# Sample attention and output mix in one block, with page numbers read earlier and the output weights in freed page strips

## The reference

```
p = rmsnorm(x) @ w_in                      # conv input, q, 3 x (k, v), gates
conv = silu(layernorm(depthwise_conv31(glu)))
o = g0 * compressed_attention(q, k_c, v_c) \
  + g1 * selected_attention(q, top-16 blocks of the paged cache, own tokens) \
  + g2 * window_attention(q, last 512 positions)
x = x + concat(rmsnorm(conv), rmsnorm(o)) @ w_out      # "mix"
h = rmsnorm(x);  x = x + hier_moe(h)                    # 4 groups x 8 experts, top 2
y = rmsnorm(x)
```

## Time and profile before

| | us |
|---|---|
| median of three runs | 1673.9 |
| profiled execution, its own time | 1674.98 |
| its span | 1672.9 |
| TensorE busy in the span | 1410.1 (84%) |
| DVE / ACT / POOL busy | 671.6 / 372.2 / 204.6 |
| sample attention block, from its first matmul | 713.80 to 787.81 |
| mix block | 789.97 to 959.93 |
| DMA over the span | 203 GB/s from and to HBM |

### The profile page before, as it was taken

One profiled execution on the slowest core, in us unless ns is written; L12 is line 12 of the kernel. 1 busy time (PEld: TensorE's weight loads), 2 busy tenths in 40 slices (PEclk: granted clock), 3 DMA queues, 4 the chain that ended last, 5 costly groups with the idle time before them and its releaser, 6 DMA issues. The chain is left out here.

```text
span 1672.9 us, 22422 instructions
## 1 busy us (share of the span) xinstructions
PE 1410.1 (84%) x7518; PEld 829.5 (50%) x7518; DVE 671.6 (40%) x1315; ACT 372.2 (22%) x802; POOL 204.6 (12%) x363
## 2 busy tenths in 40 slices
PE   5999999679899888863799806999999999999950
PEld 4665444479556656633355504544455444544420
DVE  3497788520588777661122391111011101111008
ACT  4000111331456554531011200111111111111103
POOL 0000111462400000042000001111111111111101
PEclk9999999879589999976799957999999999999985
DMA  8500000383430000064311025999999999999917
GB/s 275 226 13 1 19 16 19 128 293 113 152 102 2 2 1 2 1 177 121 148 63 64 33 119 215 402 405 405 402 398 402 405 396 387 395 396 390 398 38 287
DMA packets 81239, 326.63 MB, mean 195 GB/s; under 512 B 12319, under 2 KB 46240, under 8 KB 63042
## 3 DMA queue, kind: packets, MB, share of 16 engines
q1 hardware_dynamic: 65130, 287.51, 43.8%
q0 software_dynamic: 15952, 38.14, 6.6%
q10 hardware_dynamic: 80, 0.01, 0.0%
HBM read 310.95 MB, written 29.45 MB: 203 GB/s over the span
## 5 line engine op out<-in xcount | busy, mean ns | idle before, releaser
L1976 PE MATMUL ps<-arena 128*128 128x512 f32 x544 | 240.3, 598 | 0.0
L1976 PEld LDWEIGHTS ps<-arena 128*128 128x128 f32 x544 | 102.1, 190 | 137.2 <-issue 137.1
L540 DVE SCALAR_TENSOR_TENSOR arena<-arena 128x1024 f32<-128x1024 f32 x120 | 147.5, 1283 | 1.2
L373 PE MATMUL ps<-arena 128*128 128x512 f32 (+1 forms) x384 | 141.2, 527 | 0.0
L1637 PE MATMUL ps<-arena 128*128 128x512 f32 x256 | 115.6, 605 | 15.0 <-DVE arena L1752 15.0
L1984 PE MATMUL ps<-arena 128*64 128x256 f32 x1088 | 121.2, 380 | 0.0
L327 PE MATMUL ps<-arena 128*128 128x352 f32 x384 | 116.8, 465 | 3.3 <-issue 2.9
L2028 PE MATMUL ps<-arena 128*128 128x512 f32 x272 | 119.6, 591 | 0.0
L1112 ACT ACTIVATE arena<-ps,arena 128x640 f32<-128x640 f32 (+7 forms) x128 | 89.8, 701 | 111.1 <-DVE arena L1189 104.2
L1017 PE MATMUL ps<-arena 128*128 128x128 f32 x528 | 88.5, 292 | 20.4 <-DVE arena L1207 9.8
L373 PEld LDWEIGHTS ps<-arena 128*128 128x128 f32 x384 | 72.0, 189 | 67.1 <-issue 61.6
(11 more groups left out here) (369 smaller groups left out, 1584.2 us busy)
## 6 DMA issues: line engine op xcount, KB each, us to landing
arena<-in_w_gate SPq DMA_DIRECT2D x34, 2048.0 KB, 9.4
arena<-in_w_up SPq DMA_DIRECT2D x34, 2048.0 KB, 13.9
arena<-in_w_down SPq DMA_DIRECT2D x34, 2048.0 KB, 13.5
arena<-in_x_prompt SPq DMA_DIRECT2D x16, 512.0 KB, 6.5
arena<-in_cache_cmp SPq DMA_DIRECT2D x64, 128.0 KB, 5.7
arena<-in_cache_cmp POOLq DMA_DIRECT2D x64, 128.0 KB, 5.7
arena<-in_cache_sel SPq DMA_DIRECT2D x64, 128.0 KB, 2.5
arena<-scratch_y SPq DMA_DIRECT2D x16, 512.0 KB, 5.9
```

The source lines that it names most:

```text
L373: mm = pe.matmul(ps[:n, b + o // 512, 0:w], xT[:, k, t * P:t * P + n], w_tm[:, k, o:o + w], start=(k == 0), stop=(k == KT_ - 1))
L540: ins = dve.scalar_tensor_tensor(o, i, dw[:, c, j:j + 1], o, ALU.mult, ALU.add)
L1976: mm = pe.matmul(ps[:, bank, :], xgT_l[:, k, :], w[LARGE][:, k, :], start=(k == 0), stop=(k == KT_ - 1))
```

## The change

Sample attention and mix become one block. `reuse_semaphores()` moves from between them to the boundary ahead of the prompt attention, and SP waits for `own_block` at the end of the block before that. SP and POOL read the page numbers of half 1 at the end of their streams in the prompt attention block and keep them in registers (`late_places`). In the sample part, the `earlier` table is loaded first, the window pages in two DMAs (keys, values), 12 of the 16 pages of `spare_values` at the start, and the values of sequence 3 by both SP and POOL. On TensorE, `scores(1, c)` and `win_scores(1)` come before `sel_values(0)`; PSUM banks change accordingly.

`w_out` is now stored as strips of 128 columns: the second half in the key strips of pages 32 to 63, issued by SP once all scores of half 1 are done (ahead of the last window values and the values of sequence 3), the first half in the value strips of pages 0 to 31, issued after these. `mixT` and `hT` lie in key strips of pages 0 to 31, and `mix` takes `k` in the order 4 to 7, 0 to 3. `ln2` and `ln_final` have semaphores of their own; the first is waited for before the first `h`, the second at the end. The turning and normalising of the sample tokens' attention rows (`turn_sample`, `last_att`, `last_norm`) goes into the mix loop at tiles 0, 2 and 3. The old mix block's functions are otherwise the same and stand in the new block.

```diff
@@ -252,9 +252,10 @@
     return [eng.value_load(page_row[0:1, first + q:first + q + 1], min_val=0, max_val=cache.shape[0] - 1)
             for q in range(PAGES)]
 
-def load_pages(eng, cache, places, into, event, part=slice(0, 256)):
-
-    for q, place in enumerate(places):
+def load_pages(eng, cache, places, into, event, part=slice(0, 256), which=range(PAGES)):
+
+    for q in which:
+        place = places[q]
         eng.dma_start(into(q), cache[bass.ds(place, 1)].rearrange("a p n -> (a p) n")[:, part])\
@@ -693,6 +694,7 @@
         sp.dma_start(own_block, a["consts"][:, o:o + w]).then_inc(sem("own_block_in"), 16)
         cmp_pages(sp, 2, 0)
         cmp_pages(sp, 3, 0)
+        sp.wait_ge(sem("own_block_in"), 16)
 
     @block.tensor
     def _(pe):
@@ -848,6 +850,8 @@
 
 
 
+reuse_semaphores()
+
 att = flat(A4, TILES * 512).rearrange("p (t n) -> p t n", n=512)
 probs = flat(A2b, 3072)
 pT = flat(A3, 3072).rearrange("p (s n) -> p s n", s=3)
 
+late_places = {}
+
 with nc.Block() as block:
     @block.sync
     def _(sp):
         for b in range(4):
             load_pages(sp, a["cache_sel"], page_places(sp, a["cache_sel"], b * PAGES),
                        lambda q, b=b: pages[:, PAGES * b + q, :], f"sel_page{b}")
+        for b in (2, 0, 3):
+            late_places["sp", b] = page_places(sp, a["cache_sel"], HALF + b * PAGES)
 
     @block.tensor
             load_pages(pool, a["cache_sel"], places, lambda q: early_keys(b, q), f"sel_keys{b}", slice(0, P))
+            if b == 1:
+                late_places["pool", 1] = places
+        for b in (2, 3):
+            late_places["pool", b] = page_places(pool, a["cache_sel"], HALF + b * PAGES)
 
     @block.scalar
 CMP_AT, OWN_AT = 0, 64
-WIN_BANK, SMALL_BANK, RANK_BANK, ROW_BANK = 4, 5, 6, 7
+SMALL_BANK, RANK_BANK, ROW_BANK = 5, 6, 7
+WIN_BANK = (4, 6)
 OUT_BANK = (4, 5)
-turned_to = (0, 1, 2, 3, 6, 7)
+turned_to = ((0, 1, 2, 3, 6, 7), (0, 1, 2, 3, 6, 4))
...
+w_out_to = [pages[:, 0:32, P:2 * P], pages[:, 32:64, 0:P]]
+mixT = pages[:, 0:16, 0:P].rearrange("p (s k) n -> p s k n", s=2)
+hT = pages[:, 16:32, 0:P].rearrange("p (s k) n -> p s k n", s=2)
+xt = flat(A1 + 16384, 2048).rearrange("p (s n) -> p s n", s=2)
+h_sb = flat(A3 + 2048, 2048).rearrange("p (s n) -> p s n", s=2)
...
+def w_out(k, o, n):
+
+    return w_out_to[k // 4][:, 8 * (k % 4) + o // P:8 * (k % 4) + (o + n) // P, :]
+
...
+        def load_w_out(part):
+            sp.dma_start(w_out_to[part], a["w_out"][512 * part:512 * part + 512]
+                         .rearrange("(p c) (s m) -> p (c s) m", c=4, m=P)).then_inc(sem(f"w_out_in{part}"), 16)
...
         o, w = const_at["earlier"]
         sp.dma_start(earlier.rearrange("p i j -> p (i j)"), a["consts"][:, o:o + w])\
           .then_inc(sem("earlier_in"), 16)
+        for part in range(2):
+            sp.dma_start(win_pages[:, :, P * part:P * part + P],
+                         a["state_win_use"][0:16, :, P * part:P * part + P].rearrange("s p n -> p s n"))\
+              .then_inc(sem(f"win_page{part}"), 16)
         sp.dma_start(att_g, a["norm_att"].partition_broadcast(P)).then_inc(sem("att_gain_in"), 16)
-        places = page_places(sp, a["cache_sel"], HALF + 2 * PAGES)
         sp.wait_ge(sem("s_scored"), 4)
-        load_pages(sp, a["cache_sel"], places, lambda q: pages[:, 2 * PAGES + q, 0:P], "sel_keys2", slice(0, P))
-        places = page_places(sp, a["cache_sel"], HALF)
+        load_pages(sp, a["cache_sel"], late_places["sp", 2], lambda q: pages[:, 2 * PAGES + q, 0:P], "sel_keys2",
+                   slice(0, P))
         sp.wait_ge(sem("s_win_scored"), 1)
         sp.dma_start(win_pages[:, :, 0:P], a["state_win_use"][16:32, :, 0:P].rearrange("s p n -> p s n"))\
-          .then_inc(sem("win_page"), 16)
-        load_pages(sp, a["cache_sel"], places, lambda q: pages[:, q, 0:P], "sel_values0", slice(P, 2 * P))
-        places = page_places(sp, a["cache_sel"], HALF + 3 * PAGES)
+          .then_inc(sem("win_page0"), 16)
+        load_pages(sp, a["cache_sel"], late_places["sp", 0], lambda q: pages[:, q, 0:P], "sel_values0",
+                   slice(P, 2 * P))
+        sp.wait_ge(sem("s_scored"), 8)
+        load_w_out(1)
         sp.wait_ge(sem("sampled"), 1)
         sp.dma_start(win_pages[:, :, P:2 * P], a["state_win_use"][16:32, :, P:2 * P].rearrange("s p n -> p s n"))\
-          .then_inc(sem("win_values"), 16)
-        load_pages(sp, a["cache_sel"], places, lambda q: pages[:, 3 * PAGES + q, P:2 * P], "sel_values3",
-                   slice(P, 2 * P))
+          .then_inc(sem("win_page1"), 16)
+        load_pages(sp, a["cache_sel"], late_places["sp", 3], lambda q: pages[:, 3 * PAGES + q, P:2 * P],
+                   "sel_values3", slice(P, 2 * P), range(8))
+        load_w_out(0)
+        load_x(0)
+        sp.dma_start(ln2_g, a["ln2"].partition_broadcast(P)).then_inc(sem("ln2_in"), 16)
+        load_x(1)
+        sp.dma_start(w_router, a["w_router"].rearrange("p (k n) -> p k n", k=KT_)).then_inc(sem("w_router_in"), 16)
+        sp.dma_start(final_g, a["ln_final"].partition_broadcast(P)).then_inc(sem("final_gain_in"), 16)
...
     @block.gpsimd
     def _(pool):
-        places = page_places(pool, a["cache_sel"], HALF + 3 * PAGES)
+        def load_values2(which):
+            load_pages(pool, a["cache_sel"], late_places["pool", 2], lambda q: spare_values[:, P * q:P * q + P],
+                       "sel_values2", slice(P, 2 * P), which)
+
+        load_values2(range(0, 12))
         pool.wait_ge(sem("s_scored"), 4)
-        load_pages(pool, a["cache_sel"], places, lambda q: pages[:, 3 * PAGES + q, 0:P], "sel_keys3", slice(0, P))
-        places = page_places(pool, a["cache_sel"], HALF + 2 * PAGES)
-        load_pages(pool, a["cache_sel"], places, lambda q: spare_values[:, P * q:P * q + P], "sel_values2",
-                   slice(P, 2 * P))
-        places = page_places(pool, a["cache_sel"], HALF + PAGES)
-        load_pages(pool, a["cache_sel"], places, lambda q: pages[:, PAGES + q, 0:P], "sel_values1",
-                   slice(P, 2 * P))
+        load_pages(pool, a["cache_sel"], late_places["pool", 3], lambda q: pages[:, 3 * PAGES + q, 0:P],
+                   "sel_keys3", slice(0, P))
+        load_pages(pool, a["cache_sel"], late_places["pool", 1], lambda q: pages[:, PAGES + q, 0:P],
+                   "sel_values1", slice(P, 2 * P))
+        load_values2(range(12, 16))
+        pool.wait_ge(sem("sampled"), 1)
+        load_pages(pool, a["cache_sel"], late_places["pool", 3], lambda q: pages[:, 3 * PAGES + q, P:2 * P],
+                   "sel_values3_pool", slice(P, 2 * P), range(8, 16))
 
...
-            by_batch(half, WIN_BANK, 0, 512, lambda b: win_pages[:, 4 * b:4 * b + 4, 0:P])\
+            pe.wait_ge(sem("win_page0"), 16 * (half + 1))
+            by_batch(half, WIN_BANK[half], 0, 512, lambda b: win_pages[:, 4 * b:4 * b + 4, 0:P])\
                 .then_inc(sem("s_win_scored"), 1)
 
...
                 for b in range(4):
-                    pe.wait_ge(sem(f"sel_values{b}"), 16 * PAGES)
-                pe.wait_ge(sem("win_values"), 16)
+                    pe.wait_ge(sem(f"sel_values{b}"), 16 * (PAGES if b < 3 else 8))
+                pe.wait_ge(sem("sel_values3_pool"), 16 * 8)
+            pe.wait_ge(sem("win_page1"), 16 * (half + 1))
             terms = [(spT[:, j], lambda b, j=j: half_values(half, b, j)) for j in range(PAGES)]
             values(half, 0, terms + [(spT[:32, OWN_SEL], lambda b: v_new[:32, 0, :])])
             terms = [(spT[:, PAGES + j], lambda b, j=j: win_pages[:, 4 * b + j, P:2 * P]) for j in range(4)]
...
         small_scores()
         scores(0, 0)
-        scores(0, 1)
         importance()
-        scores(0, 2)
-        scores(0, 3)
+        for c in range(1, 4):
+            scores(0, c)
+        win_scores(0)
         spread_flags()
-        win_scores(0)
         pe.wait_ge(sem("mask_ready"), 1)
         for n in range(6):
             turn(0, n)
-        sel_values(0)
+        for n in range(6):
+            turned_copied(0, n)
         for c in range(4):
             scores(1, c)
+        win_scores(1)
+        sel_values(0)
+        for n in range(4):
+            turn(1, n)
         turn_rows(0)
-        win_scores(1)
-        for n in range(6):
-            turn(1, n)
+        turn(1, 4)
+        turn(1, 5)
         sel_values(1)
...
+            for k in (4, 5, 6, 7, 0, 1, 2, 3):
+                if t == 0 and half == 0 and k % 4 == 0:
+                    pe.wait_ge(sem(f"w_out_in{k // 4}"), 16)
+                mm = pe.matmul(ps[:n, 2 + half, :], mixT[:, t % 2, k, 0:n], w_out(k, 512 * half, 512),
+                               start=(k == 4), stop=(k == 3))
...
+        pe.wait_ge(sem("att_normed"), NQ)
+        turn_mix(0)
         turn_rows(1)
-        pe.wait_ge(sem("sample_out_copied"), 2)
-        for r in range(R):
-            mm = pe.transpose(ps[:32, ROW_BANK, r * P:(r + 1) * P], att_sT[:, r, :], ident)
-        mm.then_inc(sem("sample_turned"), 1)
```

(81 more changed lines are left out.)

269 lines of the change are left out of this document (98 added, 171 removed).

## The result

The changed kernel takes 1643.7 us (median of 4 runs, 1642.6 to 1646.3) beside 1674.45 us for the kernel before in the same runs: a ratio of 0.9817, 95% interval 0.9805 to 0.9829. The forecast was 1639, its own range 1636 to 1645. In a second set of five runs (a0_again) it took 1643.95 us, ratio 0.9816 [0.9802, 0.9829]. The profiled execution took 1646.34 us.

The account below looks back on a forecast made before the run. Sample block and mix start were taken as bound by two DMA waits, one per block, not by engine work. 34.6 + 2.65 - 0.6 - 1.7 = 35.0 us gained, so 1639 from a median of 1673.9; range 1636 to 1645, wider 1631 to 1651.

Parts of the forecast that it names:

- 34.6: Sample block up to the first mix: it starts at 772.3 on the old time axis, not 806.94, 34.6 us gained.
- Read-ahead and bytes: Sample block: without page-number reads, 13.11 MB at 285 GB/s set `sel_values(1)`: 762.0 on the old axis, 764 in the trace.
- Rival (b): Sample block DMA: at 230 GB/s `sel_values(1)` starts at 772, the mix at 782.3; 25 us gained, 1649; chance 0.21.
- costs nothing: New TensorE order: `sel_values(0)` ends 4 us later, at no cost while the DMA backlog holds, until 754.
- The 7.4 us charged for `w_out` ahead of the values: SP queue: `w_out`'s second half, 2.097 MB at 285 GB/s, holds up the last values by 7.4 us.
- Rival (a): Sample block DMA: small pieces faster (306 GB/s) or `w_out` yields; `sel_values(1)` near 757, 5 us more gained, 1634; chance 0.20.
- To the first mix: From `sel_values(1)`, 8.28 us, through turns of 1.11 us and copy of 0.9 us; the mix at 774 in the trace.
- Clock of the first mix: First mix: TensorE comes to it at a higher clock, 7.1 us instead of 9.75; 2.65 us gained.
- Moved boundary: Boundary before the prompt attention: semaphore clearing moves there and adds 1.7 us.
- Strips, `turn_sample`, the last tile's work: Mix loop: strips cost 0 (at most 4.7 us), `turn_sample` at most 0.61 us, `last_att` and `last_norm` 1.3 us if uncovered.
- Rival (c): Mix loop: strips slow each of 256 full steps; at 0.16 us a step the time is 1680; chance 0.04.
- Last stage unchanged: Stretch from the mix to the end: nothing edited, same length, 0 us; a changed length would show the prediction wrong.

Follow-up runs that it names:

- e1: The changed kernel with five of the six blocks of page numbers read in the sample block again; 1660.2 us, 0.9922 of the kernel before.
- e8: The kernel before with only the page numbers of half 1 read ahead; 1656.6 us, 0.9903 of the kernel before.
- e2: The changed kernel with the old TensorE and DVE order, values of half 0 before scores of half 1; 1645.4 us, 0.983 of the kernel before.
- e3: The changed kernel with `w_out`'s second half issued behind the last values, not ahead of them; 1640.3 us, 0.9797 of the kernel before.
- f1: The changed kernel with 32 one-column memsets on POOL in the prompt attention; 1642.5 us, 0.981 of the kernel before.
- f3: e6_filler with only one strip of each of `w_out`'s two loads; 1605.2 us in one run, a time that is not comparable.
- f4_last_and_pad: e3 with 32 one-column memsets on POOL in the prompt attention; 1640.3 us, 0.9793 of the kernel before.
- e6_filler: The changed kernel with 13 matmuls without use on TensorE ahead of `sel_values(1)`; 1647.9 us, 0.9834 of the kernel before.

## Why the prediction was right, and where it was off

The sum, term by term, against the first trace of the kernel before (us gained; the first column is the prediction's, the others the first trace and a0_again):

| | sum | first trace | a0_again |
|---|---|---|---|
| block start (moved boundary) | -1.7 | +0.5 | 0.0 |
| from block start to the first mix | +34.6 | +32.5 | +33.1 |
| the first mix itself | +2.65 | +1.0 | +2.6 |
| from its end to the plan | -0.6 | -0.8 | -0.8 |
| up to the plan | 35.0 | 33.2 | 34.9 |
| last stage | 0 | -4.9 | -4.5 |

The plan at 925.57 in a0_again, for 925.5 by the sum, is partly luck: 34.6 is 1.5 too much, and the 1.7 for the boundary were not due. The time lies inside the range, but the range was made from DMA rates, which did well, and no part of it was for the last stage, which took most of the distance to 1639.

*Read-ahead and bytes (`sel_values(1)` at 764).* Measured 763.15 and 763.04; counted from the block start 49.8 and 49.2 us, for 48.2 in the prediction. 13.11 MB at 285 GB/s was a fair price, some 5% too fast: the windows have 280 and 261 GB/s, 270 in the mean, with 291, 305 and 215 in single stretches. Rival (b) lived in the last of these, for a few us. e1 and e8 show the reads as the first cause, e2 that the order has no part in it. The prediction had that as well ("costs nothing" as long as the backlog holds), and e3 shows the condition at work: it is `w_out` that fills the gap. The 7.4 us charged for `w_out` ahead of the values were 4 to 5. Rival (a) falls for the changed kernel; in e3, where `w_out` is moved and does not yield by itself, its 757 comes nearly true and its 306 GB/s do not (279 and 249 over the stretches from 713 to 733 and 733 to 757).

*To the first mix (774).* Measured 773.93 and 773.82, with a fetch hole of 0.94 and 0.46 us inside, which the prediction did not know; the turns 1.23 for 1.11. From the start of `sel_values(1)` to the mix it is 10.8 us in both traces, for 10.3.

*Clock of the first mix (7.1 us).* It took 7.13 us in a0_again, e1, e2, f1 and f3 and 8.73 us in the first trace, where the granted clock fell as the mix began:

```profile
772.00:773.90 1.90, 1.43 (x9) 1.05 (x9) 1.77 (x5) 0.60 (x1) 0.00 (x0) 0.96 1.03 401
773.90:778.00 4.10, 4.07 (x6) 1.89 (x7) 0.28 (x2) 0.00 (x0) 0.00 (x0) 0.60 0.32 126
778.00:782.60 4.60, 4.60 (x12) 1.88 (x11) 0.00 (x0) 0.00 (x0) 0.00 (x0) 1.00 0.00 0
```

The term of 2.65 us is right in its size and comes in some executions only. The three traces with a slow first mix (8.73, 8.74, 9.71 us) are those in which TensorE had stood still for 0.94 us or more in `sel_values(1)`; after 0.46, 0.29 or no hole it took 7.13. So the fetch hole seems to cost its own length and the clock behind it; no run changes the one without the other, and this link is not shown as a cause.

*Moved boundary (+1.7).* TensorE's idle time at the start of the prompt attention went from 1.09 to 2.29 us: +1.2. But the sample block started at 713.3, not at 715.5. The boundary ahead came 0.7 us earlier (0.05 in a0_again, whose sample block started at 713.85), and the prompt attention from its first matmul to DVE's first instruction behind it took 296.5 and 296.4 us for 297.5, at the higher granted clock seen under f4_last_and_pad. That the added reads would cost nothing there was right; that they would go with a gain of 1 us could not be read from the rows.

*Strips, `turn_sample`, the last tile's work.* Products of 7.06 and 7.14 us against 7.03 and 7.11, tiles of 17.42 us against 17.37. From the end of the first mix to the plan it is 144.6 us in both traces for 143.8 in all four of the old block, 0.8 for the 0.6 of the sum. Rival (c) is excluded: the 4% of the earlier trace rows were not a price of the strips.

*Last stage unchanged.* This is the step that failed: the sum had nothing for it, and by the prediction's own signs ("if the last stage changes its length") it was wrong here. From the plan to the end it is 717.3 and 716.9 us against 712.4 and 713.7, some 4 us. The other traces narrow it: 712.4 to 713.9 in the six with 811 instructions of POOL ahead of the loop, 714.9 to 717.3 in the seven complete kernels with fewer, 3 us apart in the mean. The 2.2 us of the tail are shown to come from the number of POOL's instructions ahead of its loop: 62.51 or 62.52 us with 811, in five kernels with the old block or the new one, 64.70 to 64.95 with fewer. The 32 memsets alone undo it, wherever they stand, and e8, which has the old block and its memory layout but fewer instructions, has it too. The loop's own code did not change. The Trainium skill (Runtime: NRT & Kernel Launch, "Instruction fetch mechanics") says that engines fetch their program in blocks, and that a branch out of the fetched window costs a fetch. By it, the place of the loop would decide; but the DMA view of this stretch shows no instruction packet in any of the fourteen traces, so the mechanism behind the 2.2 us is not shown, only that it goes with the number of POOL's instructions ahead of the loop. The same section has the fetch as mostly hidden; e6_filler with 3.86 us and f3_short_w_out without it show when it is not. The other 2 us are ahead of the second round after the plan (83.9 and 83.6 for 82.6 and 83.5) and in the final block (47.1 and 47.0 for 45.7 and 46.1). Over all traces these stretches lie between 81.6 and 84.2 and between 45.0 and 47.4, so this part is spread rather than effect.

## What to carry to other kernels

Reads of page numbers into registers just ahead of their DMAs leave holes in which the DMA engines run dry; where they can be read earlier, the time of the whole stage becomes nearly bytes over rate. Then what stands ahead of the needed bytes in the same queue counts, and the compute order counts for nothing as long as the queue has other bytes to move: look for the next hole before you reorder. When two stages each wait on DMA, cost them apart: here reads and merged loads shared some 3 to 6 of 38 us. And when unedited code changes its length, count the instructions that stand ahead of its loops.

## What the runs showed of the hardware that was not expected

- An instruction fetch shares the DMA engines with data. With them full, TensorE got its next instructions 8.4 to 8.6 us after the start of `sel_values(1)` in five traces and stood still for 0.29 to 3.86 us until then, the longer the faster it had been before. With the data gone it had them in time, in 5.66 us.
- A POOL loop with skipped rounds took 13.2 or 15.4 us for the same code and the same rounds, by the number of instructions ahead of it.
- What two idle engines were given to do in the prompt attention went with TensorE's granted clock in it (0.77 to 0.88 from 450 to 500 us), and 32 memsets of 1.1 us in all stood beside a loss of 2.3 us there and of nothing in an idle stretch later.
